# GpSimd multiplies MLA's rough reciprocal with the gate; the normalisation moves behind the sixth maximum, five weight tiles are split for an MLA head

## The reference, cut to what matters

```python
# first block: "fox", 8 heads of 64, causal, with a decay f per head
# second block: MLA, 16 heads, after the projection and the norms of c_q, c_kv
q = (rmsnorm_2(c_q, q_norm) @ w_q_b).reshape(B, S, 16, 64 + 32)      # c_q 384 wide
kv = (rmsnorm_2(c_kv, kv_norm) @ w_kv_b).reshape(B, S, 16, 64 + 64)  # c_kv 256 wide
s = (q_nope @ k_nope + rope(q_rope) @ rope(k_rope)) * scale          # masked by chunks of 64
o = softmax(s) @ v                                                   # float32
y = (o * silu(z)) @ w_out                                            # z: the gate, one value per output element
```

## Time and profile before

| | before |
|---|---|
| median of 3 runs (lowest to highest) | 2225.04 us (2224.86 to 2226.74) |
| the profiled execution, its own time | 2225.34 us |
| span in its profile, mean granted TensorE clock | 2223.5 us, 0.97 |
| TensorE (PE) busy | 2064.3 us (93%) |
| VectorE (DVE) busy | 1109.1 us (50%) |
| GpSimd (POOL) busy | 1095.0 us (49%) |
| ScalarE (ACT) busy | 673.4 us (30%) |
| L1938 w_lo, all units | 173 times, 2502 ns on average |
| L1936 w_hi, all units | 173 times, 1930 ns on average |
| L684 low parts of MLA | 192 times, 1158 ns on average |

### The profile page before, as it was taken

The page is one execution under the profiler, slowest core; times in us unless marked ns, Lnnn a source line. Parts: engine busy times, 40 slices in busy tenths (PEclk is TensorE's granted clock), DMA queues, the critical chain, the costliest instruction groups (busy, mean ns, idle before and its releaser), DMA issues.

```text
span 2223.5 us, 26435 instructions
## 1 busy us (share of the span) xinstructions
PE 2064.3 (93%) x9488; PEld 1657.0 (75%) x9488; DVE 1109.1 (50%) x1189; ACT 673.4 (30%) x1085; POOL 1095.0 (49%) x651
## 2 busy tenths in 40 slices
PE   5999999989999999999999998997999999989996
PEld 3777767877788788788878876886777777768774
DVE  6545556465631212112111278314888888863576
ACT  3345564222221000000000032112666666650312
POOL 1545555414734633633443373334666666654373
PEclk9999999989999999999999998997999999989997
DMA  3100001103211211211111121111000000001122
GB/s 136 49 20 20 19 10 38 38 29 117 83 47 47 76 47 47 77 46 50 63 53 51 48 95 47 48 49 38 19 21 19 19 19 19 19 29 47 48 76 95
DMA packets 31641, 106.64 MB, mean 48 GB/s; under 512 B 3449, under 2 KB 3641, under 8 KB 31577
## 3 DMA queue, kind: packets, MB, share of 16 engines
q1 hardware_dynamic: 27520, 96.14, 13.1%
q10 hardware_dynamic: 4066, 9.74, 1.2%
HBM read 101.51 MB, written 4.26 MB: 48 GB/s over the span
## 4 chain that ended last, share of the span: by engine, by line
PE 66%; POOL 10%; DVE 10%; issue 10%; ACT 3%; ACTq 0%; DMA 0%; POOLq 0%; DVEq 0%
PE ps L225 49%; POOL probs_lo L684 7%; PE ps L390 4%; PE ps L242 3%; PE ps L254 2%; POOL w_lo L1938 2%; POOL w_hi L1936 1%; DVE h_lo L371 1%; PE ps L628 1%; DVE tmp L1764 1%; DVE x L1766 1%; PE ps L635 1%; DVE S_all L1296 1%; PE ps L629 1%; PE ps L616 1%
## 5 line engine op out<-in xcount | busy, mean ns | idle before, releaser
L1936 POOL TENSOR_TENSOR w_hi<-w_raw,zero 128x1024 fp32r<-128x1024 f32 (+1 forms) x173 | 333.9, 1930 | 820.6 <-PE ps L225 579.5
L1938 POOL TENSOR_TENSOR w_lo<-w_raw,w_hi 128x1024 fp32r<-128x1024 f32 (+1 forms) x173 | 432.9, 2502 | 13.6
L225 PE MATMUL ps<-h_hi,w_lo 128*128 128x512 f32 x1328 | 334.8, 394 | 5.3 <-DVE x L517 5.1
L225 PE MATMUL ps<-h_hi,w_hi 128*128 128x512 f32 x1328 | 328.0, 389 | 0.0
L225 PE MATMUL ps<-h_lo,w_hi 128*128 128x512 f32 x1216 | 300.4, 389 | 0.0
L225 PEld LDWEIGHTS ps<-h_hi,w_lo 128*128 128x128 f32 x1328 | 249.4, 189 | 60.3 <-issue 9.3
L684 POOL TENSOR_TENSOR probs_lo<-probs,mla_p_hi 128x512 fp32r<-128x512 f32 x192 | 218.2, 1158 | 150.2 <-ACT probs L677 150.2
L225 PEld LDWEIGHTS ps<-h_hi,w_hi 128*128 128x128 f32 x1328 | 249.2, 188 | 51.8
L225 PEld LDWEIGHTS ps<-h_lo,w_hi 128*128 128x128 f32 x1216 | 228.4, 188 | 47.7
L1378 DVE TENSOR_TENSOR tmp<-ps,tmp 128x1024 f32<-128x1024 f32 x22 | 26.9, 1224 | 370.3 <-PE ps L225 363.6
L719 DVE TENSOR_REDUCE mx<-ps 128x1 f32<-128x128 f32 (+1 forms) x192 | 137.4, 751 | 79.8 <-PE ps L660 48.9
(11 more groups left out here) (341 smaller groups left out, 3738.4 us busy)
## 6 DMA issues: line engine op xcount, KB each, us to landing
w_raw<-in_wpack SPq DMA_DIRECT2D x173, 512.0 KB, 3.2
x<-in_xT ACTq DMA_DIRECT2D x16, 512.0 KB, 7.9
out<-result SPq DMA_DIRECT2D x8, 512.0 KB, 2.9
p_raw<-in_pT ACTq DMA_DIRECT2D x1, 1024.0 KB, 6.8
pos_i<-in_pos SPq DMA_DIRECT2D x1, 512.0 KB, 6.4
const_stage<-in_consts SPq DMA_DIRECT2D x1, 404.0 KB, 3.5
vec<-in_vecs SPq DMA_DIRECT2D x1, 284.0 KB, 4.4
mla_q_hi<-c_neg ACTq DMA_DIRECT2D x16, 4.0 KB
```

What stands on the lines that cost most here:

```text
L225: last = nc.tensor.matmul(dst[:, half, :], w[slot][:, kt, :], a[:, i, t], start=(n == 0), stop=(n == total - 1))
L1936: nc.gpsimd.tensor_tensor(w_hi[s][:, kts, :], raw[s][:, kts, :], no_change[:, kts, :], ALU.add).then_inc(w_hi_done, 1)
L1938: nc.gpsimd.tensor_tensor(w_lo[s][:, kts, :], raw[s][:, kts, :], w_hi[s][:, kts, :].bitcast(F32), ALU.subtract)\
```

## The change

It does four things.

1. rough_act writes r0 to the partitions of the head's parity (64b to 64b+63) instead of always 0 to 63, and newton lies there too.
2. In MLA GpSimd multiplies r0 with the gate into rec (gate_pool): for half 0 behind low part 7, for half 1 behind low part 11, each with a wait for r0 ahead and a wait for its own result behind. On VectorE L712 is gone in exchange, and L708 computes rec = (newton - 2) * rec, having waited for the gate. So VectorE has three instructions a half in place of four. Fox keeps its three.
3. Half 0's normalisation stands on VectorE behind maximum 5 instead of behind maximum 3, in fox and in MLA.
4. The split of an MLA head's unit covers tiles 0 to 4 instead of all 8. The unit split in the last MLA step (the first one of the output weights) and fox's units keep 8.

The diff, without the semaphore's declaration and the parity arguments of the calls:

```diff
+        NORM_AFTER = 5
+        GATE_AFTER = {7: 0, N_PIECES - 1: 1}
...
-            nc.scalar.activation(r0[0:HD, :], ln_sum[0:HD, :], ACT.Exp, scale=-1.0).then_inc(A.r0_done, 1)
+            nc.scalar.activation(r0[HD * b:HD * b + HD, :], ln_sum[0:HD, :], ACT.Exp, scale=-1.0).then_inc(A.r0_done, 1)
+        def gate_pool(pool, A, n, b, half, tile, g):
+
+            pool.wait_ge(A.p_lo_done, n * N_PIECES + (g + 3))
+            pool.wait_ge(A.r0_done, n * 2 + (half + 1))
+            rows = slice(HD * b, HD * b + HD)
+            z = flat(mix[rows, bass.ds(tile, 1), half * HALF:(half + 1) * HALF])
+            nc.gpsimd.tensor_tensor(rec[rows, :], r0[rows, :], z, ALU.mult).then_inc(A.gate_done, 1)
+            pool.wait_ge(A.gate_done, n * 2 + (half + 1))
 
-            steps = 3 if gate else 2
-            seq = n * (2 * steps) + half * steps
+            seq = n * 4 + half * 2
             rows = slice(HD * b, HD * b + HD)
             if half == 1 or not (isinstance(n, int) and n == 0):
                 dve.wait_ge(A.newton, seq)
                 dve.wait_ge(A.norm_done, n * 2 + half)
-            nc.vector.tensor_tensor(newton[0:HD, :], PS[HD:P, O_BANK[half], :], r0[0:HD, :], ALU.mult).then_inc(A.newton, 1)
+            nc.vector.tensor_tensor(newton[rows, :], PS[HD:P, O_BANK[half], :], r0[rows, :], ALU.mult).then_inc(A.newton, 1)
             dve.wait_ge(A.newton, seq + 1)
-
-            nc.vector.scalar_tensor_tensor(rec[rows, :], newton[0:HD, :], -2.0, r0[0:HD, :], ALU.add, ALU.mult).then_inc(A.newton, 1)
+            if gate:
+                dve.wait_ge(A.gate_done, n * 2 + (half + 1))
+            nc.vector.scalar_tensor_tensor(rec[rows, :], newton[rows, :], -2.0, (rec if gate else r0)[rows, :], ALU.add, ALU.mult)\
+                .then_inc(A.newton, 1)
             dve.wait_ge(A.newton, seq + 2)
             dst = flat(mix[rows, bass.ds(tile, 1), half * HALF:(half + 1) * HALF])
-            if gate:
-                nc.vector.tensor_tensor(rec[rows, :], rec[rows, :], dst, ALU.mult).then_inc(A.newton, 1)
-                dve.wait_ge(A.newton, seq + 3)
             nc.vector.scalar_tensor_tensor(dst, PS[0:HD, O_BANK[half], :], -1.0, rec[rows, :], ALU.mult, ALU.mult).then_inc(A.norm_done, 1)
...
-                if i == 3 and prev is not None:
+                if i == NORM_AFTER and prev is not None:
...
+        MLA_KTS = (QL + KVL) // P
...
-            def heads(A, first):
-
-                def step(n, b, turn):
+            def heads(A, first, kts):
+
+                def step(n, b, turn, k=slice(0, kts)):
                     u = first + b + 1
-                    split(turn * 2 + u, u % 2, turn * 16 + (u // 2 * 16 + 16))
+                    split(turn * 2 + u, u % 2, turn * 16 + (u // 2 * 16 + 16), k)
                     if not (isinstance(n, int) and n == 0):
                         for g in range(N_PIECES):
                             low_pool(pool, A, n - 1, g)
-                steps(pool, A, step)
+                            if A is mla and g in GATE_AFTER:
+                                gate_pool(pool, A, n - 1, 1 - b, GATE_AFTER[g], turn - (b == 0), g)
+                last = A.heads // 2 - 1
+                for b in range(2):
+                    step(b, b, 0)
+                with pool.Fori(1, last) as turn:
+                    for b in range(2):
+                        step(turn * 2 + b, b, turn)
+                step(2 * last, 0, last)
+                step(2 * last + 1, 1, last, slice(0, DT))
                 for g in range(N_PIECES):
                     low_pool(pool, A, A.heads - 1, g)
+                    if A is mla and g in GATE_AFTER:
+                        gate_pool(pool, A, A.heads - 1, 1, GATE_AFTER[g], last, g)
             units(0, U_FQK + 1)
             fox_constants_pool(pool)
-            heads(fox, U_FQK)
+            heads(fox, U_FQK, DT)
             units(U_FQK + FOX_H + 1, U_DN[-1])
             units(U_DN[-1], U_MIN, MLP_CHUNKS[-1])
             units(U_MIN, U_HEAD + 1)
             mla_constants_pool(pool)
-            heads(mla, U_HEAD)
+            heads(mla, U_HEAD, MLA_KTS)
```

More of the change, by code:

```diff
@@ L554, in __init__ @@
                 self.newton = sem(f"{k}_newton")
+                self.gate_done = sem(f"{k}_gate_done")
                 self.norm_done = sem(f"{k}_norm_done")
@@ L685, in low_pool, with rough_act @@
                 .then_inc(A.p_lo_done, 1)
-        def rough_act(act, A, n, half):
+        def rough_act(act, A, n, b, half):
             act.wait_ge(A.pv_done, n * N_PIECES + (LAST_OF_HALF[half] + 1 + 4))
@@ L810, in step_act @@
                 if g == 6 and prev is not None:
-                    rough_act(act, A, prev, 0)
+                    rough_act(act, A, prev, 1 - b, 0)
             if prev is not None:
-                rough_act(act, A, prev, 1)
+                rough_act(act, A, prev, 1 - b, 1)
             max_row_act(act, A, n, b, turn)
@@ L819, in last_act @@
                 if g == 6:
-                    rough_act(act, A, A.heads - 1, 0)
+                    rough_act(act, A, A.heads - 1, 1, 0)
                 if split is not None and g >= N_PIECES - 2:
@@ L823, in last_act @@
                     split(g - (N_PIECES - 2))
-            rough_act(act, A, A.heads - 1, 1)
+            rough_act(act, A, A.heads - 1, 1, 1)
             if split is not None:
```

## The result

| | before | after |
|---|---|---|
| median of 4 runs each (lowest to highest) | 2225.31 us (2224.86 to 2226.74) | 2239.26 us (2234.88 to 2239.65) |
| span of the profiled execution, mean granted clock | 2223.5 us, 0.97 | 2237.0 us, 0.967 |

The ratio is 1.0062, with a 95% interval of 1.005 to 1.0075: the changed kernel is slower by 0.6%, some 14 us. The forecast had slower, but 5 us, and the time lies 1.3 us above its range. One of the ten executions of e4 (3378 us, granted clock 0.56) and one of the six of e8 (8103 us, 0.24) were in a slow state and are in none of the ratios.

The account below looks back on a forecast made before the run. In the MLA heads it saw TensorE 91% busy at clock 1.00, waiting for VectorE's maxima and GpSimd's low parts. Terms -6.0 +3.2 +7.0 +1.0 = +5.2 us on the 2225.04 us median gave 2230, range 2219 to 2238.

Parts of the forecast that it names:

- three signs of being wrong: Fox heads keeping their length, MLA heads shrinking by a microsecond, or L1687 still starting behind low part 0.
- part 3: Fox heads: normalisation before maxima 6 and 7 delays the closing transposes, +1.0 us a head, +7.0 us over 7 heads.
- Part 1: End of an MLA head: rope product comes ahead of low part 0, -0.43 us a head, -6.0 us over 14 heads.
- sentence on the five tiles: MLA split: five tiles by themselves shorten nothing that is waited for, but make Part 1 possible; no gain of their own.
- Part 2: Middle of an MLA head: wait for maximum 4 exchanged for one on GpSimd's queue, +0.21 us a head, +3.2 us.
- Part 4: Behind the last head: later gate and low part 8, L712 gone, split taking turns; +1 us, bounds -2 and +3.
- (c): Rival, middle of MLA head: wait before L658 goes, nothing replaces it, needing a 0.5 us gate; -16, 2209; chance 0.17.
- (d): Rival, MLA: the gate costs 1.9 us or each gate loses a further turn, 2239 us; chance 0.13.

Follow-up runs that it names:

- e4: The kernel before with five tiles split in MLA and the gate product on GpSimd for half 1 alone, normalisation behind maximum 3: 2220.61 us, ratio 0.9986.
- e8: The changed kernel with fox's normalisation behind maximum 3 and half 0's MLA gate ahead of low part 7: 2217.22 us, ratio 0.9968.
- e5: The kernel before with the five-tile split of the MLA heads alone: 2217.68 us, ratio 0.9972.
- e2: The changed kernel with three unneeded matmuls filling the waits for maxima 6 and 7 in fox heads from the second on: 2238.64 us, ratio 1.0069.
- e6: The changed kernel with the normalisation behind maximum 3 in fox and MLA and half 0's gate ahead of low part 7: 2217.60 us, ratio 0.997.
- e1: The kernel before with only half 0's normalisation moved behind maximum 5, in fox and MLA: 2261.79 us, ratio 1.0184.
- e9: Against e5, MLA's normalisation of half 0 behind maximum 5, with the gate on VectorE: 2250.61 us, ratio 1.0113 to the kernel before.
- e3: The changed kernel with fox's normalisation back behind maximum 3, MLA keeping all of the change: 2229.86 us, ratio 1.0026.
- e7: The changed kernel with half 0's normalisation behind maximum 3 in fox and 4 in MLA, its gate ahead of low part 7: 2210.25 us, ratio 0.9938.
- e10: As e7, but half 1's gate back on VectorE, only half 0's on GpSimd: 2210.14 us, ratio 0.9935 to the kernel before.

## Why the prediction was off

The direction came out, and so did the turns of VectorE and GpSimd and the places of the new waits inside the heads, and none of the three signs of being wrong came. But the time is above the range. The step that failed is part 3, which took TensorE's granted clock of 1.00 for given and so put the clock at nothing; beside it the terms of parts 1 and 2 were mis-sized, both to the hopeful side. Together they were to shorten an MLA head by 0.22 us; it became 0.15 longer.

- **Part 1** (start of an MLA head, forecast -0.43 us a head): measured -0.28. The turns came as written: L1697 5.8 us behind the start of the last L640 (L635 before), L1700 ahead of low part 0, low part 0 held up by it (its pair ends 2.9 us after its start instead of 3.24). The term was too large by a third, 2 us over 14 heads. Its sentence on the five tiles, that by themselves they shorten nothing that is waited for, was wrong: e5 has the whole gain. The step that failed followed VectorE only with the gate in GpSimd's queue; in the kernel before L708 waits behind w_lo, and a shorter w_lo is enough.
- **Part 2** (middle, +0.21): measured +0.43. The exchange of the wait for maximum 4 against one for low part 8 is as described, the gate took 1.29 us as taken from the nearest row. What was too small are the gaps around it, 0.27 and 0.16 us: low part 8 starts 3.02 us behind low part 7 where the working has 2.8. 3.3 us over 15 heads. The estimate by the Trainium skill, page GPSIMD Engine Reference, section 3.1, 1.11 us, was too low by 0.18; by it the error would have been larger.
- **Part 3** (fox, +1.0): both waits are where they were put, and the queue costs 1.02 us in the odd heads, but 1.3 in the even ones (e2, and the second head here), 8.0 us in all where the sum had 7.0. The stage lost 12.1. **The missing cause is TensorE's clock**: in two heads it fell to 1.2 GHz for 3.4 us, which cost 1.5 us each, 3.0 together, and 1.1 us more in the first head, where it rose 2.9 us later, as it does in e6 without the change. The forecast priced idle time at its own length. The link between the waits and the falls is shown in fox by e2; in MLA e1 and e9 have it. The Trainium skill (page TensorE: Matmul & The Clock Gate, Part 1) gives 426.7 ns from start to start for 512 columns at 1.2 GHz and some 216 at 2.4; the trace has 0.40 to 0.43 us from 227.54 on and 0.23 from 231.26 on, so it agrees on what a fall costs. How much idle time brings a fall on, no row of the kernel before could have told.
- **In MLA** a fall of the clock added 2.6 us in the profiled execution (two heads), 0 in the sum. e2 and e3, with the same MLA heads, have one and two falls, in other heads, and the kernel before, e4, e5, e6, e7 and e10 none behind the stage's start. What brings them on in the changed kernel, whose only wait of over 0.4 us in a head is the 1.01 us for low part 8, is not shown.
- **Part 4** (tail, +1.0): measured -2.3 us, 0.3 beyond the lower of its bounds. That the split would take turns with the mix_lo tiles held; that the clock would be at its lower level for 3 us less was not foreseen.
- The rivals: (c), low part 8 not late, did not happen in the changed kernel, and against the forecast's sentence it does not need a gate of 0.5 us. (That no two-input GpSimd row is that short holds for 512 elements; a low part of 128 takes 0.46 us.) It needs another place for the gate: e7's heads are 0.5 us shorter than e5's that way (26.0 against 26.5 on average, 26.86 before). (d) had the right time, 2239 (its own terms give 2240), for the wrong reason: the gate took 1.29 us and not 1.9.

The forecast of +5.2 and what it missed, in the profiled execution: clock in fox +4.1, fox queue +1.0, clock in MLA +2.6, part 2 +3.3, part 1 +2.0, tail -3.3, and -1.3 in the first MLA head, which began with 3.0 us at the lower clock instead of 5.3, are together +8.4. With the 5.2 that makes 13.6, near the 13.5 measured.

```profile
1550.80:1556.10 5.30, 5.30 (x15) 4.15 (x15) 1.57 (x3) 0.00 (x0) 0.00 (x0) 0.50 0.21 81
```

```profile
1562.80:1565.80 3.00, 3.00 (x9) 2.42 (x9) 1.57 (x3) 0.00 (x0) 0.00 (x0) 0.50 0.00 0
```

The first row is the stretch at the lower clock in that head before, the second after.

What stays open: how much of the median the clock makes up. It falls at other places from execution to execution (the stages between fox and MLA, which no variant touches, took 1229.7 to 1234.1 us). The four runs of the changed kernel reach from 2234.9 to 2239.7; the fastest has a mean granted clock of 0.972, the others 0.967 or 0.968. And e2, which removed the falls in fox from the profile, did not lower the median.

## What to carry to other kernels

Moving work behind a wait on a shared queue frees that wait and delays everything that was behind it: follow the queue to the last instruction that another engine needs, as the maxima that close a head here. Added work on a second engine is free only where that engine idles before the work, so look for its idle row and put it there. And on a TensorE that is kept busy throughout price a new idle time not only at its length, but also at what it may cost if the clock falls for it; moving idle time to where other waits are can do that even if its sum stays the same, as e9 has it.

## What the runs showed of the hardware

Idle times of 0.5 and 0.26 us at the end of a head, on top of 1.2 us in its middle, were followed by 3.4 us at 1.2 GHz in two of seven fox heads (three of seven in e1); with the same waits filled by three matmuls there was none. With idle times of 1.2 and 0.26 us at the end of each MLA head (e9) the mean clock was 0.91 from 1600 to 1930 us, where e5 has 1.00, though TensorE idles hardly more in a head than before. A move that costs 1.3 us by the queue cost 2.8 in two fox heads.

VectorE's instructions with two inputs in SBUF and GpSimd's take turns by whole instructions in the rows shown: L722 took 1.54 and 1.58 us beside w_hi and low part 8, L708 0.69 us in e5 where nothing ran beside it.
